# A hybrid decoder layer on one core: gate projections as fp32 products inside the attention loop, through DRAM, with three score banks

## The chip, the core and the metric

The kernel runs on one core of a Trainium2 chip. TensorE (PE) multiplies, VectorE (DVE), ScalarE (ACT) and GpSimd (POOL) do the rest, SyncE (SP) issues most of the DMA transfers. The engines run their own instruction queues in order and wait for each other on semaphores. The metric is the device time of one execution in microseconds; lower is better.

## The reference

One layer, 1024 tokens of width 1024, fp32. Two parts, each behind a modulated RMS norm and with a residual around it:

```python
# mixer: three attentions on h, merged by gates of every channel
q_a, kv_a, gate_a, qkv_b, q_c, kv_c, merge = split_cols(h @ w_in, IN_WIDTHS)
o_a = nsa_attention(...)      # 8 heads: compressed + selected + 512-token window
o_b = stick_breaking(...)     # 4 heads, all earlier keys
o_c = swa_with_sinks(...)     # 4 heads, 128-token window
g = jax.nn.sigmoid(merge).reshape(B, S, N_BRANCH, D)
y = g[:, :, 0] * (o_a @ w_branch_a) + g[:, :, 1] * (o_b @ w_branch_b) + g[:, :, 2] * (o_c @ w_branch_c)
return y @ w_out
# then: top-2 of 16 experts per token (router, gather, silu(x @ w_gate) * (x @ w_up) @ w_down, weighted sum)
```

`merge` is the product of h (1024 x 1024) with 3072 columns of w_in: the gate projection, of which this change speaks.

## The kernel before

The kernel is one program with an order written out by hand for each engine. Its stages follow each other on TensorE:

- **Projections** (0 to 337 us): norms, modulation, q, k and v of all heads. The normed tokens stay in SBUF as `hT`.
- **The attention loop** (337 to 1031 us). Queries are worked in 8 tiles of 128 tokens (n = 0 to 7). A tile has 20 units: 8 window heads (`win`, at most 5 key blocks of 128), 8 selected heads (`slc`, n+1 blocks) and 4 sliding-window heads (`swa`, at most 2 blocks). Each unit has a *slot*; 6 slots drain the loop, so there are 166. Four `sb` heads per tile (n+1 blocks) *ride* in slots 6, 9, 12 and 15, and a `cmp` unit (compressed keys) opens the tile. In slot q TensorE makes the scores of its unit and of its ride (L1631, masks L1633), then the transposes (L1660) of the unit of slot q-1 and of the ride of slot q-4, and value products (L1692) one unit behind these. VectorE takes the row maximum (L1224), ScalarE the exponential (L871), both copy the transposed probabilities out of PSUM (L387, L389). VectorE gathers a tile's output in slots 5, 10 and, for the tile before, 2 (L1196 to L1208). Scores use two PSUM buffers of two banks (512 columns each) in turn (`score_buf`, L348): a unit's scores wait until those of two units earlier have been read.
- **The mix** (1031 to 1416 us), 48 groups r = 6m + 2b + half: for 128 output channels m, branch b and half of the tokens, the gate projection and the branch product. fp32 tokens and weights of the gate are split into a high and a low fp32r part by ScalarE and VectorE (`tokens_hi`, L435; `weights_hi`, L447; L440 and L452), and TensorE makes lo*hi + hi*lo + hi*hi: 24 products a group (L1728). The branch product is plain fp32, 4 or 2 products (L1733). ScalarE's sigmoid (L908), VectorE's product and sum (L1293 to L1299) follow. The weights come in 8 loads, one per m (`loads`, from `L_MIX` on).
- **Output projection** (to 1557 us): x and the first expert weights are loaded by SP behind the mix (L565, L576), products L1758, then x1 and the second norm (L1312 on).
- **Routing** (to 1627 us): the plan of blocks, the table `slot_tok` by 16 scattering DMAs (L744) of GpSimd. SP fills the unused rows of `y_dram` with copies of x in a loop over `n_spare` (L594; 8 of them here, for 24 blocks).
- **Experts** (1627 to 2108 us), a loop over 16 experts and inside it over their blocks of 128 tokens. All products are split in three as above (L1791 to L1793 gate and up, L1831 to L1836 down). ScalarE makes the high parts of the next expert's weights (L934, six halves), VectorE the low parts (L1407, six halves); TensorE's first gate product of an expert waits for both low halves of the gate weights (L1811). After its splits VectorE copies the last block's result (L1420), then ScalarE does silu (L964) and VectorE the product with up (L1438), which is transposed (L1819).
- **Tail**: rows gathered from `y_dram`, weighted, added to x1, stored.

## Time and profile before

| | us |
|---|---|
| median of 3 runs (2157.27 to 2161.97) | 2158.88 |
| the profiled execution | 2160.99 |
| its span, first to last instruction | 2159.4 |
| attention loop, 337 to 1026: TensorE busy | 606.29 of 689 |
| mix, 1040 to 1417: TensorE busy | 375.38 of 377 |
| experts, 1627 to 2108: TensorE busy | 446.67 of 481 |

Times in rows are microseconds from the start of the span, or durations in microseconds. PE is TensorE's matmul, PEld its weight load. L is a line of the kernel. A row of a timeline names start, length, engine, line, operation, output<-input and count; behind it in brackets the idle time of that engine before it and what ended it. PEclk is the clock that was granted to TensorE as a share of 2.4 GHz; it knows that level and half of it. An fp32 product is two matmul instructions, an fp32r product one.

### The profile page before, as it was taken

To read this page: it belongs to the slowest core of one execution; us is meant where nothing else is said; L and a number is where in the kernel's file an instruction comes from. 1 tells how busy PE (TensorE), PEld (TensorE's weight loads), DVE (VectorE), ACT (ScalarE), POOL (GpSimd) and SP (SyncE) were. 2 spreads that over 40 slices of the span, in tenths; PEclk is the share of its full clock that TensorE was granted. 3 is DMA by queue.
4 is the path that set the end of the run, shared out by engine and by line. 5 is a ranking of instruction groups with operands and counts; after the bars stand their busy time and mean duration, and the time that the engine had idled before them with its cause. 6 is when DMAs were issued, how large, how long until landed. Compare 5 with 4: busy or idle time off the path is not lost.

```text
span 2159.4 us, 22519 instructions
## 1 busy us (share of the span) xinstructions
PE 1864.6 (86%) x8189; PEld 1337.2 (62%) x8189; DVE 968.5 (45%) x1519; ACT 667.7 (31%) x1168; POOL 239.3 (11%) x277
## 2 busy tenths in 40 slices
PE   2999998788989898989799999989808999999990
PEld 2554646666667676767577777745506777777770
DVE  5554314545445364645422222123353566466575
ACT  1311103333424252525311111100124445354551
POOL 3211310000101010202000000000040000000002
PEclk9999996666777696969899999999958999999995
DMA  9244310000000000000112211163344667586758
GB/s 342 101 156 137 76 43 1 1 1 1 1 1 1 1 1 1 1 1 1 39 39 65 53 40 39 40 235 114 105 131 175 226 232 280 187 308 246 267 191 321
DMA packets 119362, 226.64 MB, mean 105 GB/s; under 512 B 6888, under 2 KB 45888, under 8 KB 119136
## 3 DMA queue, kind: packets, MB, share of 16 engines
q1 hardware_dynamic: 107744, 189.50, 26.0%
q0 software_dynamic: 7920, 22.72, 3.0%
q10 hardware_dynamic: 3600, 13.11, 1.5%
q8 instruction: 61, 1.00, 0.2%
q14 instruction: 37, 0.30, 0.0%
HBM read 199.60 MB, written 29.91 MB: 106 GB/s over the span
## 4 chain that ended last, share of the span: by engine, by line
PE 73%; DVE 14%; ACT 4%; issue 4%; DMA 3%; POOL 1%; SPq 1%; ACTq 0%; DVEq 0%; POOLq 0%
PE psum L1728 12%; PE psum L1631 9%; PE psum L1532 8%; PE psum L1692 7%; PE psum L1733 5%; PE psum L1791 4%; PE psum L1793 4%; PE psum L1792 4%; PE psum L1660 4%; PE psum L1758 4%; DVE arena_r L1407 3%; PE psum L1552 3%; ACT heads_r L934 1%; DVE negm L1224 1%; POOL slot_tok L744 1%
## 5 line engine op out<-in xcount | busy, mean ns | idle before, releaser
L1692 PE MATMUL psum<-kv,arena 128*128 128x64 f32 x1464 | 229.9, 309 | 59.9 <-DVE arena L1208 36.1
L1692 PEld LDWEIGHTS psum<-kv,arena 128*128 128x128 f32 x1464 | 223.0, 231 | 67.7 <-issue 38.1
L1728 PE MATMUL psum<-arena_r,kv_r 128*128 128x512 f32 x768 | 238.3, 391 | 0.0
L1631 PE MATMUL psum<-kv,heads 112*128 112x512 f32 (+7 forms) x384 | 194.4, 620 | 9.9 <-DVE arena L1232 9.1
L1532 PE MATMUL psum<-arena 128*128 128x512 f32 (+2 forms) x512 | 187.7, 520 | 0.0
L1224 DVE TENSOR_REDUCE negm<-psum 128x1 f32<-128x640 f32 (+7 forms) x128 | 90.5, 707 | 213.0 <-PE psum L1633 212.6
L1791 PE MATMUL psum<-arena_r,kv_r 128*128 128x512 f32 x384 | 154.9, 403 | 33.9 <-DVE arena_r L1407 31.7
L1728 PE MATMUL psum<-arena_r 128*128 128x512 f32 x384 | 169.9, 442 | 9.5 <-DVE arena_r L452 9.5
L871 ACT ACTIVATE arena<-psum,negm 128x640 f32<-128x640 f32 (+7 forms) x128 | 89.7, 701 | 281.6 <-DVE negm L1224 279.9
L1660 PE MATMUL psum<-ident,arena 128*128 128x128 f32 x828 | 158.7, 321 | 15.5 <-ACT arena L387 8.9
L1728 PEld LDWEIGHTS psum<-arena_r,kv_r 128*128 128x128 f32 x768 | 145.0, 189 | 41.0 <-issue 11.2
L1793 PE MATMUL psum<-heads_r,kv_r 128*128 128x512 f32 x384 | 153.4, 399 | 0.0
L1792 PE MATMUL psum<-heads_r,kv_r 128*128 128x512 f32 x384 | 153.1, 399 | 0.0
L1407 DVE TENSOR_TENSOR arena_r<-arena,heads_r 128x2048 fp32r<-128x2048 f32 x64 | 142.4, 2287 | 15.2 <-ACT heads_r L934 15.1
L722 POOL TENSOR_SCALAR arena<-arena 128x128 f32<-128x128 f32 (+7 forms) x32 | 76.4, 2389 | 602.1 <-ACT arena L894 602.1
L1532 PEld LDWEIGHTS psum<-arena 128*128 128x128 f32 x512 | 95.5, 191 | 75.9 <-issue 73.0
L1660 PEld LDWEIGHTS psum<-ident,arena 128*128 128x128 f32 x828 | 112.9, 172 | 47.7 <-issue 20.9
L908 ACT ACTIVATE kv<-psum 128x512 f32<-128x512 f32 x48 | 28.7, 597 | 323.1 <-PE psum L1728 323.1
L934 ACT ACTIVATE heads_r<-arena 128x2048 fp32r<-128x2048 f32 x64 | 117.2, 1913 | 2.5 <-DMA arena<-in_w_exp_up_dram 1.6
L1733 PE MATMUL psum<-heads,arena 128*128 128x512 f32 x256 | 117.6, 591 | 0.0
L1758 PE MATMUL psum<-arena,bc 128*128 128x512 f32 x256 | 112.5, 599 | 2.7 <-issue 2.7
L1631 PEld LDWEIGHTS psum<-kv,heads 112*128 112x128 f32 (+1 forms) x384 | 80.7, 251 | 47.8 <-issue 35.8
(347 smaller groups left out, 2696.1 us busy)
## 6 DMA issues: line engine op xcount, KB each, us to landing
arena<-in_w_exp_gate_dram SPq DMA_DIRECT2D x16, 2048.0 KB, 9.4
arena<-in_w_exp_up_dram SPq DMA_DIRECT2D x16, 2048.0 KB, 11.9
arena<-in_w_exp_down_dram SPq DMA_DIRECT2D x16, 2048.0 KB, 10.1
arena<-in_w_ada_dram SPq DMA_DIRECT2D x7, 2048.0 KB, 15.4
y_dram<-bc ACTq DMA_DIRECT2D x25, 512.0 KB, 2.7
arena<-in_w_in_dram SPq DMA_DIRECT2D x24, 512.0 KB, 5.3
bc<-in_w_ada_dram SPq DMA_DIRECT2D x4, 2048.0 KB, 8.1
arena<-in_w_in_dram SPq DMA_DIRECT2D x3, 2048.0 KB, 11.7
```

Source lines behind the costliest of these rows:

```text
L934: act.activation(ew_hi[i][:, cs], w_raw(e, i)[:, cs], ACT.Copy).then_inc(w_hi_ok, 1)
L1407: dve.tensor_tensor(ew_lo(e, i)[:, cs], w_raw(e, i)[:, cs], ew_hi[i][:, cs].bitcast(F32), ALU.subtract).then_inc(w_lo_ok, 1)
L1532: mm = pe.matmul(psum[:, 4 + s % 3, 0:w], hT[:, k, n * P:(n + 1) * P], slot(slot_of(L_TOK + ch))[:, k, 0:w], start=(k == 0), stop=(k == NK ...
L1631: mm = pe.matmul(b[:, c0:c1], lhs, keys[:, k0 + c0:k0 + c1], start=True, stop=not masks)
L1660: ins = pe.transpose(bank[:, c * P:(c + 1) * P], src[:, t * P:(t + 1) * P], ident[:, :])
L1692: mm = pe.matmul(psum[:, bank, c * HD:(c + 1) * HD], pt[:, j * P:(j + 1) * P], v, start=(j == 0), stop=(j == u["nb"] - 1))
L1728: mm = pe.matmul(psum[:, 2 * (r % 4), :], w, h, start=(k == 0 and i == 0), stop=(k == NK - 1 and i == 2))
L1733: mm = pe.matmul(psum[:, 2 * (r % 4) + 1, :], mix_branch(s)[:, k, :], oT[:, hf * 4:(hf + 1) * 4, k, :], start=(k == k0), stop=(k == k1 - 1))
L1758: mm = pe.matmul(psum[:, 2 * (n % 2) + h, :], yT[:, k, n * P:(n + 1) * P], slot(slot_of(L_OUT + h))[:, k, :], start=(k == 0), stop=(k == N ...
L1791: pe.matmul(out, lhs_hi[:, k, :], rhs_lo(k), start=(k == 0), stop=False)
L1792: pe.matmul(out, lhs_lo[:, k, :], rhs_hi(k), start=False, stop=False)
L1793: mm = pe.matmul(out, lhs_hi[:, k, :], rhs_hi(k), start=False, stop=(k == n - 1))
```

## The change

1. **Gate projections in the loop.** The 48 gate groups are made as plain fp32 products, 8 per group, no split. `gate_steps(q)` spreads them: from slot 2 on, three slots make one group with 3, 3 and 2 products, at the end of TensorE's slot; the last group ends in slot 145. They use PSUM bank 3; ScalarE copies it to `z_stage` at the end of its slot, SP stores it to `z_dram`. Weights (512 KB per pair of groups) are loaded by SP in three buffers.
2. **Three score banks.** Bank 3 being taken, scores have banks 0 to 2. Units of up to 4 blocks take the bank used longest ago, `cmp` bank 2, larger ones banks 0 and 1 together; each waits for the last users of its banks. The ride's scores move behind the transposes and values of their slot.
3. **The mix** has branch products alone; their weights and the first half of w_out are loaded during the loop. z comes back from DRAM six groups at a time (1.5 MB) into two buffers, ScalarE makes the sigmoid of all six at once. The second half of w_out is loaded behind the loop.
4. **Expert passes** (`project_tokens`): for gate and up first all products with high weights, waiting for high halves, then those with low weights, waiting for low halves; down waits for low halves one by one.
5. **Spare rows.** All 33 blocks of `y_dram` are filled by SP during the loop; ScalarE waits for that before its first store.
6. Some semaphores go; `res_in` is shared by two loads.

```diff
+                big = u["kind"] != "cmp" and u["n"] + 1 - u["lo"] > 4
+                rest = [2] if u["kind"] == "cmp" else [min((0, 1, 2), key=lambda b: bank_user[b])]
+                u["banks"] = [0, 1] if big else rest
+                u["after"] = sorted({bank_user[b] for b in u["banks"]} - {-1})
+                for b in u["banks"]:
+                    bank_user[b] = n_s
...
         def score_buf(u):
-            return psum[:, 2 * (u["s"] % 2):2 * (u["s"] % 2) + 2, :].rearrange("p a b -> p (a b)")
+            return psum[:, u["banks"][0]:u["banks"][-1] + 1, :].rearrange("p a b -> p (a b)")
...
+        N_GATE, FILL0 = 3 * 2 * NK, 2
+        GATE_BANK = psum[:, 3, :]
+        gate_w = [part_of(0, i * NK * P, (i + 1) * NK * P).rearrange("p (k n) -> p k n", k=NK) for i in range(3)]
+        z_stage = [part_of(0, 3 * NK * P + i * BANK, 3 * NK * P + (i + 1) * BANK) for i in range(2)]
+        gate_in, branch_in = [sem(f"gate_in{i}") for i in range(3)], [sem(f"branch_in{i}") for i in range(2)]
+        g_full, z_ok = sem("g_full"), sem("z_ok")
+        z_out, z_in = [sem("z_out0"), sem("z_out1")], [sem("z_in0"), sem("z_in1")]
+
+        def gate_steps(q):
+
+            g, c = divmod(q - FILL0, 3)
+            return (g, ((0, 1, 2), (3, 4, 5), (6, 7))[c]) if 0 <= g < N_GATE else (g, ())
+
+        def branch_w(m):
+            a = m % 4 * NK * P
+            return part_of(4 + m // 4, a, a + NK * P).rearrange("p (k n) -> p k n", k=NK)
+
+        def z_group(m):
+            return part_of(2 + m % 2, 0, 6 * BANK)
...
+        z_dram = nc.dram_tensor("z_dram", [NK, P, 6 * BANK], F32, kind="Internal").ap()
...
-            load(L_MIX)
+
+            def load_gate(t):
+                m, b = divmod(t, 3)
+                sp.dma_start(gate_w[t % 3], win[:, :, C_MERGE + b * D + m * P:C_MERGE + b * D + (m + 1) * P]
+                             ).then_inc(gate_in[t % 3], 16)
+
+            sp.wait_ge(hid_full, 1)
+            for t in range(3):
+                load_gate(t)
             sp.dma_start(wr[:, :, :], w_router.rearrange("(k p) e -> p k e", p=P)).then_inc(wr_in, 16)
             sp.dma_start(rbias[:, :], router_bias.partition_broadcast(P)).then_inc(wr_in, 16)
 
+            for g in range(N_GATE):
+                sp.wait_ge(z_ok, g + 1)
+                sp.dma_start(z_dram[g // 6, :, g % 6 * BANK:(g % 6 + 1) * BANK], z_stage[g % 2]).then_inc(z_out[g % 2], 16)
+                if g % 2 and g // 2 + 3 < N_GATE // 2:
+                    load_gate(g // 2 + 3)
+                if g <= N_BLK:
+                    sp.dma_start(y_dram[g * P:(g + 1) * P, :], x2d[0:P, :]).then_inc(spare_out, 16)
+            for m in range(NK):
+                for w, k0, k1 in ((w_branch_a, 0, 4), (w_branch_b, 4, 6), (w_branch_c, 6, 8)):
+                    sp.dma_start(branch_w(m)[:, k0:k1, :], w.rearrange("l (k p) n -> p (l k) n", p=P)[:, :, m * P:(m + 1) * P]
+                                 ).then_inc(branch_in[m // 4], 16)
+            for i in range(2):
+                sp.wait_ge(z_out[i], 8 * N_GATE)
+            load(L_OUT)
+
+            def load_z(m):
+                sp.dma_start(z_group(m), z_dram[m]).then_inc(z_in[m % 2], 16)
+
             sp.wait_ge(t_full, n_g)
-            for i in range(L_MIX + 1, len(loads)):
-                load(i)
+            sp.wait_ge(pv_done, n_v)
+            load_z(0)
+            load_z(1)
+            load(L_OUT + 1)
+            for m in range(2, NK):
+                sp.wait_ge(mix_done, 6 * (m - 1))
+                load_z(m)
 
             def load_expert(e, i):
                 w = (wge, wue, wde)[i]
                 sp.dma_start(as_k(w_raw(e, i), i), w[e]).then_inc(expert_w[3 * (e % 2) + i], 16)
 
-            wait_used(sp, L_OUT - 1)
...
-            n_spare = sp.value_load(plan_i[0:1, 2 * NE + 1:2 * NE + 2], min_val=1, max_val=N_BLK - NE)
-            with sp.Fori(0, n_spare) as j:
-                sp.dma_start(y_dram[bass.ds(N_BLK * P - j * P, P), :], x2d[0:P, :]).then_inc(spare_out, 16)
...
+                sp.dma_start(res[n], x1_dram[n * P:(n + 1) * P, :]).then_inc(res_in[n // 2], 16)
...
-            tokens_hi(act, 0)
-            weights_hi(act, 0)
-            tokens_hi(act, 1)
-            weights_hi(act, 1)
-            for r in range(3 * 2 * NK):
-                if r % 2 == 0:
-                    weights_hi(act, r // 2 + 2)
-                act.wait_ge(mix_full, 2 * r + 1)
-                if r >= 2:
-                    act.wait_ge(mix_done, r - 1)
-                act.activation(sig[r % 2], psum[:, 2 * (r % 4), :], ACT.Sigmoid).then_inc(sig_ok, 1)
+                g, ks = gate_steps(q)
+                if NK - 1 in ks:
+                    act.wait_ge(g_full, g + 1)
+                    if g >= 2:
+                        act.wait_ge(z_out[g % 2], 16 * (g // 2))
+                    act.activation(z_stage[g % 2], GATE_BANK, ACT.Copy).then_inc(z_ok, 1)
+
+            for m in range(NK):
+                act.wait_ge(z_in[m % 2], 16 * (m // 2 + 1))
+                act.activation(z_group(m), z_group(m), ACT.Sigmoid).then_inc(sig_ok, 1)
...
+            act.wait_ge(spare_out, 16 * (N_BLK + 1))
...
+                sig = z_group(m)[:, r % 6 * BANK:(r % 6 + 1) * BANK]
+                dve.wait_ge(mix_full, r + 1)
+                dve.wait_ge(sig_ok, m + 1)
...
-                if u["s"] >= 2:
-                    wait_scores_read(pe, u["s"] - 2)
+                for i in u["after"]:
+                    wait_scores_read(pe, i)
...
+            def gate_matmuls(q):
+
+                g, ks = gate_steps(q)
+                t, hf = divmod(g, 2)
+                for k in ks:
+                    if k == 0:
+                        if hf == 0:
+                            pe.wait_ge(gate_in[t % 3], 16 * (t // 3 + 1))
+                        if g:
+                            pe.wait_ge(z_ok, g)
+                    mm = pe.matmul(GATE_BANK, gate_w[t % 3][:, k, :], hT[:, k, hf * BANK:(hf + 1) * BANK],
+                                   start=(k == 0), stop=(k == NK - 1))
+                    if k == NK - 1:
+                        mm.then_inc(g_full, 1)
+
             waiting = None
-            for s in slots:
+            for q, s in enumerate(slots):
                 for u in s["S"]:
-                    scores(u)
+                    if u is not s["ride"]:
+                        scores(u)
                 for u in s["T"]:
                     if waiting and "v" not in u:
                         values(waiting)
@@ -1705,32 +1707,25 @@
                     if waiting:
                         values(waiting)
                     waiting = u if "v" in u else None
+                if s["ride"]:
+                    scores(s["ride"])
+                gate_matmuls(q)
...
+            pe.wait_ge(z_ok, N_GATE)
             for r in range(3 * 2 * NK):
                 m, b, hf = r // 6, r // 2 % 3, r % 2
-                s = slot_of(L_MIX + m)
-                if r % 6 == 0:
-                    wait_load(pe, L_MIX + m)
+                if r % 24 == 0:
+                    pe.wait_ge(branch_in[m // 4], 16 * 12)
                 if r >= 4:
                     pe.wait_ge(mix_done, r - 3)
-                pe.wait_ge(w_rest, r // 2 + 1)
-                if r < 2:
-                    pe.wait_ge(h_rest, r + 1)
-                for k in range(NK):
-                    w_hi, w_lo = gate_hi(r // 2)[:, k, :], gate_lo(r // 2)[:, k, :]
-                    t_hi, t_lo = (h[:, k, hf * BANK:(hf + 1) * BANK] for h in (h_hi, h_lo))
-                    for i, (w, h) in enumerate(((w_lo, t_hi), (w_hi, t_lo), (w_hi, t_hi))):
-                        mm = pe.matmul(psum[:, 2 * (r % 4), :], w, h, start=(k == 0 and i == 0),
-                                       stop=(k == NK - 1 and i == 2))
-                mm.then_inc(mix_full, 1)
                 k0, k1 = ((0, 4), (4, 6), (6, 8))[b]
                 for k in range(k0, k1):
-                    mm = pe.matmul(psum[:, 2 * (r % 4) + 1, :], mix_branch(s)[:, k, :],
+                    mm = pe.matmul(psum[:, 2 * (r % 4) + 1, :], branch_w(m)[:, k, :],
...
-            def split_matmuls(out, lhs_hi, lhs_lo, rhs_hi, rhs_lo, n):
-
-                for k in range(n):
-                    pe.matmul(out, lhs_hi[:, k, :], rhs_lo(k), start=(k == 0), stop=False)
-                    pe.matmul(out, lhs_lo[:, k, :], rhs_hi(k), start=False, stop=False)
-                    mm = pe.matmul(out, lhs_hi[:, k, :], rhs_hi(k), start=False, stop=(k == n - 1))
-                return mm
+            def project_tokens(i, e, w_hi, w_lo, full):
+
+                out, c0 = psum[:, i, :], 6 * e + 2 * i
+                for k in range(NK):
+                    if k % 4 == 0:
+                        pe.wait_ge(w_hi_ok, c0 + k // 4 + 1)
+                    pe.matmul(out, xs_hi[:, k, :], w_hi[:, k, :], start=(k == 0), stop=False)
+                    pe.matmul(out, xs_lo[:, k, :], w_hi[:, k, :], start=False, stop=False)
+                for k in range(NK):
+                    if k % 4 == 0:
+                        pe.wait_ge(w_lo_ok, c0 + k // 4 + 1)
+                    mm = pe.matmul(out, xs_hi[:, k, :], w_lo[:, k, :], start=False, stop=(k == NK - 1))
+                mm.then_inc(full, 1)
...
-                    for i, full in enumerate((gate_full, up_full)):
-                        pe.wait_ge(w_lo_ok, 6 * e + 2 * i + 2)
-                        split_matmuls(psum[:, i, :], xs_hi, xs_lo, lambda k: hi[i][:, k, :], lambda k: lo[i][:, k, :],
-                                      NK).then_inc(full, 1)
+                    project_tokens(0, e, hi[0], lo[0], gate_full)
+                    project_tokens(1, e, hi[1], lo[1], up_full)
...
-                    pe.wait_ge(w_lo_ok, 6 * e + 6)
                     for k in range(4):
                         if k % 2 == 0:
+                            pe.wait_ge(w_lo_ok, 6 * e + 5 + k // 2)
```

## Rows read from the trace of the kernel before

**Rows 1.** The page: busy time, share and instructions of each engine.

```profile
PE 1864.6 (86%) x8189; PEld 1337.2 (62%) x8189; DVE 968.5 (45%) x1519; ACT 667.7 (31%) x1168; POOL 239.3 (11%) x277
```

**Rows 2.** Table of stretches: length, busy us (count) by engine, PEclk, DMA, GB/s.

```profile
337.00:1026.00 689.00, 606.29 (x3228) 465.97 (x3228) 340.72 (x703) 274.24 (x640) 78.24 (x40) 0.77 0.00 1
1040.00:1417.00 377.00, 375.38 (x1415) 266.57 (x1416) 85.47 (x104) 50.40 (x71) 0.00 (x0) 1.00 0.16 40
1627.00:2108.00 481.00, 446.67 (x2016) 360.11 (x2016) 282.41 (x259) 237.73 (x239) 36.67 (x48) 0.98 0.65 236
```

**Rows 3.** Waits in the loop: us in total, times, longest.

```profile
PE psum L1692 <- DVE arena L1208: 36.1, 7, 5.3
PE psum L1692 <- DVE arena L389: 23.8, 19, 2.8
```

**Rows 4.** Tile 6: a timeline row, then a stretch as in rows 2.

```profile
819.31 2.37 PE L1692 MATMUL psum<-kv,arena 128*128 128x64 f32 x10 [5.27 <-DVE arena L1208]
832.00:836.00 4.00, 4.00 (x26) 3.94 (x25) 1.52 (x2) 1.05 (x3) 0.00 (x0) 0.62 0.02 6
```

**Rows 5.** Chain that ended last, in the mix: start, us, what.

```profile
1047.32 3.43 PE psum L1733 x8
1050.75 5.45 PE psum L1728 x24
```

**Rows 6.** Timeline near the loop's end, tile 7.

```profile
1014.29 1.22 DVE L1274 TENSOR_TENSOR arena<-arena 128x1024 f32<-128x1024 f32 x1
1018.06 1.23 DVE L1224 TENSOR_REDUCE negm<-psum 128x1 f32<-128x1024 f32 x1 [1.36 <-PE psum L1633]
1018.09 1.90 PE L1692 MATMUL psum<-kv,arena 128*128 128x64 f32 x16
1019.32 1.11 ACT L871 ACTIVATE arena<-psum,negm 128x1024 f32<-128x1024 f32 x1 [0.97 <-DVE negm L1224]
```

**Rows 7.** Timeline from the loop into the mix, and behind the mix.

```profile
1030.65 3.62 ACT L435 ACTIVATE arena_r<-arena 128x4096 fp32r<-128x4096 f32 x1 [0.26 <-PE psum L1660]
1040.11 0.76 PE L1728 MATMUL psum<-arena_r 128*128 128x512 f32 x1 [9.50 <-DVE arena_r L452]
1043.72 0.40 PE L1728 MATMUL psum<-arena_r 128*128 128x512 f32 x1
1422.64 29.16 PE L1758 MATMUL psum<-arena,bc 128*128 128x512 f32 x64 [2.67 <-issue]
1446.43 1.23 DVE L1312 TENSOR_TENSOR heads<-psum,ga_bc 128x1024 f32<-128x1024 f32 x1 [25.13 <-DMA kv<-in_x_dram]
```

**Rows 8.** The page's DMA issues: KB each, us to landing.

```profile
bc<-in_w_ada_dram SPq DMA_DIRECT2D x4, 2048.0 KB, 8.1
```

**Rows 9.** Timeline of the routing: scatters and splits.

```profile
1584.45 8.90 DVE L1407 TENSOR_TENSOR arena_r<-arena,heads_r 128x2048 fp32r<-128x2048 f32 x4
...
1587.92 1.86 POOL L744 DMA_INDIRECT slot_tok<-tok_id,dest  x1 [0.30 <-issue]
...
1600.16 0.96 POOL L744 DMA_INDIRECT slot_tok<-tok_id,dest  x1 [0.30 <-issue]
```

**Rows 10.** Experts: chain that ended last, then timeline.

```profile
1701.00 1.93 ACT heads_r L934
1723.13 1.93 ACT heads_r L934
1921.69 1.93 ACT heads_r L934
1942.13 1.93 ACT heads_r L934
...
1729.72 0.47 PE L1791 MATMUL psum<-arena_r,kv_r 128*128 128x512 f32 x1 [2.11 <-DVE arena_r L1407]
1739.68 0.60 ACT L964 ACTIVATE bc<-psum 128x512 f32<-128x512 f32 x1 [5.14 <-DVE bc L1420]
1740.90 0.75 DVE L1438 TENSOR_TENSOR bc<-bc,psum 128x256 f32<-128x256 f32 x2 [1.91 <-PE psum L1793]
```

85 lines of the change are left out of this document (15 added, 70 removed).

## Prediction

> **What bounds the kernel now.** I read the page first: TensorE is busy 86% of the span [rows 1]. A busy share says little about an engine whose clock changes, so the second view is the table of stretches [rows 2]. Three stretches hold 1547 of the 2159.4 us. The reader should see the pair of figures in each: in the mix (1040 to 1417) TensorE is busy 375.4 of 377 us at a granted clock of 1.00, so it is bound by the number of its products alone. In the attention loop (337 to 1026) it is busy 606.3 of 689 us, but at a mean of 0.77: it sits idle 82.7 us, and for a large part of the rest runs at the lower of its two levels. The experts (1627 to 2108) are busy 446.7 of 481 us at 0.98. So work taken out of the mix comes off the end in full, and work put into the loop can hide in two places, idle time and the slow clock.
>
> **The attention loop, as it stands.** The granted clock has two levels, 2.4 and 1.2 GHz, so busy time times mean clock is about the work at full clock: 606.3 x 0.77 = 467 us. If all the idle time fell at the lower level, the busy part would have a clock of 0.81 and the work would be 489 us; I take 467. The loss to the clock is then 606 - 467 = 139 us. The third view, the waits, says what ends the idle time: 36.1 us in 7 waits of the value products for VectorE's gather (L1208), 23.8 us for its copies out of PSUM [rows 3]; the rest is spread thin. The gather's wait is one of some 5.3 us at the start of each of tiles 1 to 7, and after it TensorE keeps the lower level for long: the 4 us from 832 on have a mean of 0.62, so it came back at about 835 [rows 4].
>
> **What the change adds to the loop.** 48 gate groups of 8 fp32 products of 512 columns are 384 products. The mix's branch products are of the same shape and type: four products of branch A are 8 instructions, so two each, and the 8 go by in 3.43 us [rows 5]. 768 instructions x 3.43/8 = 329 us at full clock. (The products they replace are 1152 single-pass ones, 24 in 5.45 us, 262 us [rows 5]: on TensorE the new form is 67 us dearer.) Loop work becomes 467 + 329 = 796 us.
> *Idle time.* The gather's waits stay (36 us): the values that wait stand in slot 2 behind that slot's scores, and the gate products are queued behind the values, in an engine that keeps its order. Of the other 47 us I let half stay: a gate step stands between the transposes of one slot and the values of the next and so covers copies, and the compressed scores have a bank of their own; waits inside a slot are not covered. The new waits: from tile 4 on a unit of more than 4 blocks takes banks 0 and 1 together, so its scores wait until the exponential of the large unit before has read them. In tile 7 the maximum starts at 1018.06 and the exponential ends at 1020.43, 2.4 us [rows 6]. The slot's values alone take 1.9 us there (its transposes come on top), and the gate step adds 8/3 x 0.86 = 2.3 us, so the chain is covered. The gate steps end with slot 145 of 166; in the last 14 loaded slots only the four ride units, whose reader comes right behind them, are bare: 4 x 1.3 = 5 us. Sum 36 + 24 + 5 = 65 us.
> *Clock.* Each slot gets 2.3 us of dense products. In the mix, after 9.5 us of idleness, dense products had the upper level back by 1043.7, in 3.6 us or less [rows 7]; in the loop it took some 15 us after 819.3 [rows 4]. I price 8 tiles at 4 us lost each, 32, and 3 for the first tile: 35 us. Bounds: 0, and 139 x 796/467 = 238 us, if the shares stay as they are. I take the low side, since a slot would be dense for a third to three quarters of its time.
> ScalarE gets 48 copies of 0.6 us and VectorE nothing; both are at half load (340.7 and 274.2 of 689 us). SyncE's queue, idle in the loop, gets stores, weight loads and 33 spare copies, about 42 MB in 800 us, behind no one's deadline: a weight buffer is read again six groups later. Loop: 796 + 65 + 35 = 896 us for 689, **+207**.
>
> **What it takes from the mix.** Before: from 1026 to 1416.1 are 390 us: the last gather and transposes until 1031, splits of tokens and weights until 1040.1 [rows 7], then the products. After: 5 us until 1031, then 256 branch instructions x 0.429 = 110 us [rows 5], 2 us for a slow start, 1.5 us for VectorE behind the last: 118.5. The read-back has to keep this up. Two z groups of 1.5 MB and a half of w_out are issued as the loop ends; 2 MB take 8.1 us to land [rows 8], and a sigmoid of 3072 columns is 3/4 of the 3.62 us of a 4096-column copy [rows 7], plus 1.3 us for its table. So VectorE starts 10 to 12 us after the loop, and TensorE has four groups (10 us) to do ahead of it. Later each buffer has 13.7 us for 8 + 2.7 us. Covered, with little to spare; if not, each group costs up to 3 us, 20 in all. Mix: **-271** (-250 if bare).
>
> **Behind the mix.** The second half of w_out was issued when the mix was through and held the first output product until 1422.6, 2.7 us after TensorE was free; x, queued behind it and four expert loads, came at 1446.4 [rows 7]. With w_out already there, both come sooner: **-6** (0 to -8).
>
> **Spare rows early.** They leave the path between routing and the experts. The scatters of slot_tok are issued there, 1.9 us each until 1598, then 0.96 [rows 9]. Two things end at about 1598: the spare copies and VectorE's six splits, which began at 1584.5 and take 13.4 us at 8.9 for four. If the copies are the cause, 7 us go; if the splits are, none: **-2** (0 to -7). [...]
>
> **Experts.** TensorE waits 2.1 us for the low halves (L1407) at each of 15 changes of expert, as at 1729.7 [rows 10], and some changes are followed by a dip of the clock: one-block experts take 22.1 us with it (1701.00 to 1723.13) and 20.4 without (1921.69 to 1942.13) [rows 10]. The new order needs only the high halves at first, so the 2.1 us go. But what is late next is VectorE: its six splits are followed by its copy of the last result, then ScalarE's silu (1739.68 to 1740.28), then the product L1438. At 1740.90 that product waited for TensorE, but silu was only some 0.6 us ahead [rows 10]. ScalarE and VectorE alone need 17.3 us from L934 (1723.13) to a ready silu (1740.3), plus 2.8 to the next L934: some 20 us for 20.4. So 0.4 us x 15 = 6, and half of the dips, of which 5 of the 14 intervals seem to hold one, at 1.7 us, 4: **-10** (-3 to -30; the full 2.1 us and all dips would be 40, but the chain excludes it). The tail is unchanged (0; +1 for the paired waits on res).
>
> **Sum.** 207 - 271 - 6 - 2 - 10 = -82. The profiled execution took 2160.99 us (span 2159.4), 2.1 above the median of the runs, so 2079 for it and **2077 us** as a median.
>
> **Rivals.**
> *A, better filled loop.* The gate steps also take most of the slow clock (10 instead of 35) and half of the remaining waits (15 less): 2077 - 40 = 2037. For it: dense work at 1.00 in the mix. Against: the gather's waits, longer than a step.
> *B, single-buffered scores, slower.* Tiles 4 to 7 have 64 + 16 large units. If VectorE is still in a scan when scores end (scan and subtraction before 1015.4 take some 3.5 us, of which the subtraction alone is 1.2 [rows 6]), the chain is not 2.4 but up to 5.9 us. It cancels the 82 us from 1.03 us a unit on; at 1.8 us it gives 2077 + 144 = 2221. Against: 5 us of TensorE work per slot between two scores in all but the last 14.
> *C, the clock does not rise.* Loss 238 instead of 35: 2280; it cancels the gain from 117 us on. Partly so (80): 2122.
> *D, the experts gain nothing or the read-back is bare*: up to +30, 2107.
> A change that does not do what it says would be an expert stage at 481 us with its waits only renamed; that is D.
>
> **How the numbers follow.** Forecast (with D) 0.67, A 0.2, C in part 0.06, C in full 0.02, B 0.05. The range reaches to A's time and to C in part with D's smaller half: 2030 to 2130; it leaves out some 0.15. A measurement of this kernel can tell about 0.2%, 4 us. Faster 0.92 (forecast, A, C in part, less 0.01), same 0.01, slower 0.07 (B and C in full).
>
> **What would show it.** Right: the loop some 207 us longer with a clock of 0.93 to 0.97 in it; gate instructions at 0.43 us; mix stretch of some 115 us with TensorE busy throughout; seven waits for L1208 still of 5 us; in the experts L1407 gone from TensorE's waits and L1438 (or its product's transposes) in its place. Wrong: waits of score products for ScalarE's L871 in tiles 4 to 7 of over 1 us (B), a clock under 0.87 in the loop (C), gaps of TensorE in the mix every 13.7 us (read-back).

## The result and the profile after

| | before | after |
|---|---|---|
| median, us | 2159.24 (2157.27 to 2161.97, 4 runs) | 2127.02 (2117.63 to 2131.74, 4 runs) |
| profiled execution, us | 2160.99 | 2127.09 |
| its span, us | 2159.4 | 2125.4 |
| attention loop | 694.2 (337.1 to 1031.3) | 946.5 (335.2 to 1281.7) |
| mix, from the loop's end | 384.8 (to 1416.1) | 113.6 (to 1395.3) |

The ratio is 0.984 (95% interval 0.9823 to 0.9856): 32 us faster where 82 were forecast. The time lies in the range given; the gain is 50 us smaller than forecast.

The page's first group of the kernel after:

```profile
PE 1852.2 (87%) x7805; PEld 1195.6 (56%) x7805; DVE 933.9 (44%) x1493; ACT 659.6 (31%) x1150; POOL 239.5 (11%) x277
```

The table of stretches of [rows 2] in the kernel after (length, busy us and count of PE, PEld, DVE, ACT, POOL, then PEclk, DMA share, GB/s):

```profile
335.00:1276.00 941.00, 859.69 (x3996) 537.34 (x3996) 342.41 (x705) 302.36 (x688) 78.62 (x40) 0.94 0.17 51
1281.00:1395.00 114.00, 111.83 (x256) 49.20 (x256) 55.41 (x81) 22.90 (x9) 0.00 (x0) 0.98 0.35 129
1601.00:2075.00 474.00, 444.77 (x2016) 363.47 (x2016) 282.83 (x259) 238.06 (x239) 36.58 (x48) 0.97 0.66 240
```

TensorE's total busy time hardly moved from [rows 1], 1864.6 to 1852.2 us, with 384 fewer instructions. The loop's row is the one to read. It is 941 us where the forecast had 896, and it still has 81 us without a product, as before (82.7, [rows 2]).

The waits of TensorE in that loop (us in total, times, longest), to be read against [rows 3]:

```profile
PE psum L1678 <- DVE arena L1199: 36.7, 7, 5.3
PE psum L1678 <- DVE arena L394: 20.0, 15, 2.1
PE psum L1646 <- ACT arena L392: 6.9, 12, 0.9
PE psum L1617 <- ACT arena L888: 5.2, 4, 1.6
PE psum L1617 <- ACT arena L865: 5.1, 4, 1.3
PE psum L1678 <- ACT arena L392: 5.1, 10, 0.7
```

L1678 are the value products (L1692 before), L1199 the gather (L1208), L394 and L392 the copies of probabilities out of PSUM by VectorE (L389) and ScalarE, L1617 the scores, L865 ScalarE's exponential and L888 its copy of a ride's scores. Both rows of before are there again almost unchanged: 36.1 became 36.7, 23.8 became 20.0. Behind them are the two new rows of L1617, 10 us in 8 waits of scores for the reader of their bank, 1.3 us each in the mean: the four of L888 are all in tile 7, those of L865 come once in each of tiles 4 to 7. Two rows of the kernel before belong beside them:

```profile
PE psum L1631 <- DVE arena L1232: 9.1, 8, 2.0
PE psum L1660 <- ACT arena L387: 8.9, 7, 1.4
```

The first is a wait of scores for VectorE's reading of the compressed scores; it is all but gone (0.6 us). The second is the wait of transposes for ScalarE's copies, 6.9 us after, with 5.1 us of value products waiting for the same copies behind it. All waits for copies together were 33.5 us and are 32.0. The last tile, where steps stand only in the first 6 of 20 slots, has the longest idle time and the lowest clock:

```profile
1137.37:1281.68 144.31, 123.84 (x663) 86.37 (x661) 62.56 (x103) 51.67 (x91) 18.31 (x12) 0.87 0.17 50
```

The stretches add up in the two profiled executions: start of the loop -2, loop +252, mix -271, output stage -3, routing -2, experts -8, tail 0, together -34 us.

### The profile page after: what moved, and what is told of

Same layout as the page of the kernel before. It is cut to its first block, busy times and chain, and to the rows that moved or that the text cites. A ratio compares the mean times of both kernels' runs of the same rounds, so it can differ in the third digit from the quotient of the medians.

```text
span 2125.4 us, 21714 instructions
## 1 busy us (share of the span) xinstructions
PE 1852.2 (87%) x7805; PEld 1195.6 (56%) x7805; DVE 933.9 (44%) x1493; ACT 659.6 (31%) x1150; POOL 239.5 (11%) x277
## 4 chain that ended last, share of the span: by engine, by line
PE 70%; DVE 16%; issue 4%; ACT 3%; DMA 3%; POOL 1%; ACTq 1%; SPq 1%; DVEq 0%; POOLq 0%
PE psum L1692 17%; PE psum L1518 9%; PE psum L1617 8%; DVE arena_r L1393 8%; PE psum L1678 7%; PE psum L1728 5%; PE psum L1753 4%; PE psum L1646 4%; PE psum L1538 3%; PE psum L1789 2%; PE psum L1790 2%; PE psum L1794 2%; ACT heads_r L924 1%; POOL slot_tok L740 1%; DVE negm L1215 1%
## 5 line engine op out<-in xcount | busy, mean ns | idle before, releaser
L1692 PE MATMUL psum<-arena 128*128 128x512 f32 x768 | 387.2, 640 | 0.5 <-ACT arena L894 0.4
L1678 PE MATMUL psum<-kv,arena 128*128 128x64 f32 x1464 | 198.1, 280 | 61.9 <-DVE arena L1199 36.7
L1678 PEld LDWEIGHTS psum<-kv,arena 128*128 128x128 f32 x1464 | 188.4, 201 | 69.5 <-issue 38.2
L1692 PEld LDWEIGHTS psum<-arena 128*128 128x128 f32 x768 | 144.7, 204 | 128.3 <-issue 128.0
L865 ACT ACTIVATE arena<-psum,negm 128x640 f32<-128x640 f32 (+7 forms) x128 | 89.6, 700 | 404.5 <-DVE negm L1215 404.5
L1617 PE MATMUL psum<-kv,heads 112*128 112x512 f32 (+7 forms) x384 | 147.9, 490 | 5.8 <-ACT arena L888 5.2
L1646 PE MATMUL psum<-ident,arena 128*128 128x128 f32 x828 | 131.3, 280 | 10.6 <-ACT arena L392 6.9
L1518 PEld LDWEIGHTS psum<-arena 128*128 128x128 f32 x512 | 95.5, 191 | 75.8 <-issue 73.0
L1617 PEld LDWEIGHTS psum<-kv,heads 112*128 112x128 f32 (+1 forms) x384 | 73.2, 202 | 90.7 <-issue 84.0
L1646 PEld LDWEIGHTS psum<-ident,arena 128*128 128x128 f32 x828 | 92.5, 146 | 41.5 <-issue 27.2
L1794 PE MATMUL psum<-arena_r,kv_r 128*128 128x512 f32 x384 | 95.0, 389 | 0.0
L1728 PEld LDWEIGHTS psum<-heads,arena 128*128 128x128 f32 x256 | 49.2, 193 | 63.2 <-issue 63.2
L1789 PEld LDWEIGHTS psum<-heads_r,kv_r 128*128 128x128 f32 x384 | 72.9, 190 | 17.8 <-DVEq L1411 2.6
## 6 DMA issues: line engine op xcount, KB each, us to landing
arena<-in_w_exp_up_dram SPq DMA_DIRECT2D x16, 2048.0 KB, 12.3
```

What stands on the lines that cost most here:

```text
L1518: mm = pe.matmul(psum[:, 4 + s % 3, 0:w], hT[:, k, n * P:(n + 1) * P], slot(slot_of(L_TOK + ch))[:, k, 0:w], start=(k == 0), stop=(k == NK ...
L1617: mm = pe.matmul(b[:, c0:c1], lhs, keys[:, k0 + c0:k0 + c1], start=True, stop=not masks)
L1646: ins = pe.transpose(bank[:, c * P:(c + 1) * P], src[:, t * P:(t + 1) * P], ident[:, :])
L1678: mm = pe.matmul(psum[:, bank, c * HD:(c + 1) * HD], pt[:, j * P:(j + 1) * P], v, start=(j == 0), stop=(j == u["nb"] - 1))
L1692: mm = pe.matmul(GATE_BANK, gate_w[t % 3][:, k, :], hT[:, k, hf * BANK:(hf + 1) * BANK], start=(k == 0), stop=(k == NK - 1))
L1728: mm = pe.matmul(psum[:, 2 * (r % 4) + 1, :], branch_w(m)[:, k, :], oT[:, hf * 4:(hf + 1) * 4, k, :], start=(k == k0), stop=(k == k1 - 1))
```

## Experiments

All were timed beside the kernel before, whose median was there between 2160.6 and 2163.6 us. Differences from the kernel after are taken from the medians of separate runs; where one is only a few us, the traces have to bear it out.

### 1. The score banks alone

The kernel before with three banks for scores instead of four and the ride's scores behind the values, and nothing else of the change:

```
- return psum[:, 2 * (u["s"] % 2):2 * (u["s"] % 2) + 2, :]
+ return psum[:, u["banks"][0]:u["banks"][-1] + 1, :]
- if u["s"] >= 2: wait_scores_read(pe, u["s"] - 2)
+ for i in u["after"]: wait_scores_read(pe, i)
```

> One part alone, on the kernel before: three score banks (large units take banks 0 and 1 together) and the ride's scores behind transposes and values; no gate products in the loop, mix and experts as before. Theory T (the loop's idle time stayed because the waits stand inside a slot, ahead of its gate step; the banks themselves cost little): the loop of 694 us grows by 10 to 20 us, with new waits of scores for L871 and L894 copies of about 1 us each in tiles 4 to 7; 2170 to 2180 us. Rival R1 (single-buffered large scores are what ate the 45 us that the loop is longer than forecast): the loop grows by 40 us or more, 2200 us.

Measured: 2189.59 us (2187.58 to 2197.0), ratio 1.0125 (1.0094 to 1.0155): 26 us slower (32 us in the profiled loops). Its loop as one stretch:

```profile
338.34:1064.60 726.26, 632.84 (x3236) 479.88 (x3236) 344.28 (x709) 274.85 (x641) 78.62 (x40) 0.75 0.00 1
```

Its waits of scores for the ride's copy (L901) and the exponential (L878):

```profile
PE psum L1638 <- ACT arena L901: 18.3, 16, 1.6
PE psum L1638 <- ACT arena L878: 4.5, 8, 0.8
```

That lies between T's 10 to 20 us and R1's 40. R1's cause, large units waiting for the exponential, is 4.5 us here and 5.1 us in the kernel after, so it is not what ate the 45 us. The same 3236 instructions as before take 632.8 us instead of 607.8: 726.3 - 632.8 = 93 us are idle, 7 more than before (86; the new waits are 23 us, but the 9.1 us for the compressed scores and some of those for copies are gone), and the other 25 lie in the busy time, at a clock of 0.75 instead of 0.77. Busy time times clock is 475 for 468 us, within what two decimals of the clock leave open, so most of the 25 us is the clock. This execution is the slowest of the four, and how much of the 25 us is its own is not shown. Without the gate products the three banks are a loss of 26 us; in the change's own loop only 10 us of such waits are left.

### 2. The banks without the ride's move

As 1, but the ride's scores at their old place:

```
- for u in s["S"]:
-     if u is not s["ride"]: scores(u)
+ for u in s["S"]: scores(u)
...
- if s["ride"]: scores(s["ride"])
```

> The kernel before with three score banks, but with the ride's scores left at their old place, ahead of the transposes (the other kernel with three banks moved them behind the slot's values, and took 2189.6 us, 26 us over the kernel before). Theory T (the number of banks is what costs: a ride must wait until the scores of a slot or two before have been read, and its place within the slot changes little): 2184 to 2196 us, about 20 waits of TensorE for the exponentials of ScalarE with some 20 us in the loop. Rival R1 (moving the ride is the cost): 2163 to 2175 us. Rival R2 (the place behind the values is what keeps the cost low: ahead of the transposes the wait is longer by the time of transposes and values, some 3 us per ride of the longer tiles): 2210 us or more.

Measured: 2209.42 us (2201.38 to 2213.27), ratio 1.0229 (1.0212 to 1.0246), 20 us above experiment 1, above T and next to R2's 2210. The waits, and the loop as one stretch:

```profile
PE psum L1638 <- ACT arena L901: 27.0, 16, 2.3
PE psum L1638 <- ACT arena L878: 9.1, 9, 1.8
...
336.22:1066.00 729.78, 617.39 (x3233) 473.65 (x3234) 344.37 (x709) 273.69 (x640) 78.21 (x40) 0.76 0.00 1
```

36 us in 25 waits instead of 23 us in 24: the place of the ride matters in R2's direction, but by 0.5 us a wait where R2 had some 3. The idle time is 112 us, 26 more than before, and the busy time 10 us more: here idle time brought less slow clock with it than in experiment 1. The profiled executions of the two are only 4 us apart (2199.7 and 2195.4 us), so of the 20 us between the medians I call only the direction and the waits shown.

### 3. A step inside the slot where the gather is awaited

The kernel after with a whole group of eight gate products in slot 2 of tiles 1 to 7, between the transposes and the values that wait for the gather; the other steps stay at the end of their slots and start again in slot 3 of each tile:

```
+ steps[t0 + 2] = (gq, tuple(range(8)))
...
+ early = last_values >= 0 and (s["i"] == 2)
+ for i, (f, u) in enumerate(calls):
+     if early and i == last_values: gate_matmuls(q)
+     f(u)
```

> The changed kernel with the gate steps redistributed: in slot 2 of tiles 1 to 7 a whole group of 8 products stands between the transposes and the values that wait for VectorE's gather; the other groups in three slots each as before; the last group is in slot 2 of tile 7. Same products, same order otherwise. Theory T: 6.9 us of products cover the wait of 5.3 us, so the seven waits for the gather (36.7 us) go, and the dips of the clock behind them too (some 3 to 4 us each): loop 50 to 60 us shorter, 2127 becomes 2070 to 2080. Rival R2 (VectorE's and ScalarE's chain behind the gather sets the tile's start, so the wait comes back one slot later): at most 10 us shorter, 2117 or more.

Measured: 2067.21 us (2063.37 to 2073.63), ratio 0.9556 (0.9527 to 0.9585): 60 us less than the kernel after, for the same instructions in another order; this is T. The seven waits of 5.3 us are gone from its list; of the gather only the wait at the loop's end is left:

```profile
PE psum L1662 <- DVE arena L1215: 3.3, 1, 3.3
...
PE psum L1694 <- DVE arena L394: 20.6, 16, 2.1
```

### 4. All steps inside their slots

As 3, and the ordinary steps too stand ahead of the slot's last values, in every slot without a ride:

```
- early = last_values >= 0 and (s["i"] == 2)
+ early = last_values >= 0 and (s["i"] == 2 or not s["ride"])
```

> This kernel is the one whose group of eight gate products stands in slot 2 of each tile ahead of the last values (it took 2067.2 us, its loop 891.7 us with 49.6 us idle on TensorE). Here the ordinary gate steps too stand ahead of the slot's last values, in every slot without a ride, where before they stood at the slot's end. Theory T (the idle time that the change left in the loop lies inside the slots, ahead of where its steps stand, so the place of a step decides and not the amount of work): of the waits for evacuated probability groups in that loop (20.6 us in 16 by VectorE, 6.9 and 5.4 us by ScalarE) about half goes, 15 to 20 us; idle in the loop 30 to 37 us, time 2045 to 2055 us. Rival R: a step ahead of the values delays the values and with them the next slot's evacuation and exponentials, so that waits come back elsewhere: idle 45 us or more, time 2064 us or more.

Measured: 2026.98 us (2025.4 to 2028.47), ratio 0.9379 (0.9363 to 0.9394): another 40 us, twice what T gave it. The wait for VectorE's copies:

```profile
PE psum L1694 <- DVE arena L394: 2.7, 3, 1.7
```

Tile 5 as a stretch, in the kernel after:

```profile
857.09:993.11 136.02, 125.55 (x617) 81.10 (x616) 51.12 (x93) 45.34 (x92) 12.56 (x4) 0.96 0.10 30
```

In experiment 3:

```profile
843.59:972.52 128.93, 123.51 (x623) 79.66 (x621) 51.14 (x93) 45.37 (x92) 12.57 (x4) 1.00 0.11 31
```

And in experiment 4:

```profile
804.25:930.30 126.05, 122.96 (x623) 80.16 (x623) 51.14 (x93) 45.03 (x92) 12.56 (x4) 1.00 0.11 32
```

The work (busy times clock) is 121, 124 and 123 us; the first has a third of a gate group less in it, 2.3 us. What goes is idle time, 10.5, 5.4 and 3.1 us. The slow clock goes with the gather's wait: the clock is 1.00 already in experiment 3, with 5.4 us of short gaps still there. Over the whole loop, each term summed tile by tile from such rows (the loss is busy time less work):

| us | loop | idle | lost to the clock | work |
|---|---|---|---|---|
| before | 694.2 | 86 | 140 | 467 |
| after | 946.5 | 85 | 52 | 810 |
| 3 | 891.7 | 50 | 31 | 811 |
| 4 | 853.3 | 26 | 25 | 803 |

Of the 93 us between the kernel after and experiment 4, 59 are idle time, 27 are clock and 7 are in the work column, which the clock's two decimals leave uncertain by about as much. In tiles 0 to 6 idle time falls from 64 to 12 us and the loss to the clock from 35 to 5. Tile 7 keeps 13 us idle and 20 us of loss; it takes 133.7 us in this execution, 127.5 in that of experiment 3 and 125.2 in that of experiment 10, which has the same loop as this one.

### 5. ScalarE's store behind the SiLU

The kernel after, with the wait for VectorE's copy of the block's result, and the store, moved behind `silu` (the order that results):

```
  act.activation(y_sb[:, BANK:D], psum[:, 6, :], ACT.Copy).then_inc(y_act, 1)
+ act.wait_ge(gate_full, j + 2)
+ act.activation(silu_g, psum[:, 0, :], ACT.Silu).then_inc(silu_ok, 1)
  act.wait_ge(y_act, j + 1)
  act.wait_ge(y_dve, j + 1)
  act.dma_start(y_dram[bass.ds(j * P, P), :], y_sb).then_inc(y_out, 16)
```

> The changed kernel, with ScalarE's store of a block's result (and its wait for VectorE's copy) moved behind silu in the experts. Theory T (ScalarE's and VectorE's chain from the high halves through six splits, VectorE's copy, silu and the product with up sets a one-block expert's 20.0 us): silu no longer follows VectorE's copy, the chain is 1.1 us shorter, one-block experts take 18.9 to 19.2 us, and with the stall of TensorE under 1 us its clock dips less: stage of 473 us becomes 450 to 458, 2127 becomes 2105 to 2112. Rival (TensorE's own work or the weights' arrival sets the period): 20.0 us stay, 2127.

Measured: 2098.73 us (2096.42 to 2102.77), ratio 0.9713 (0.9682 to 0.9745): 28 us less: T's mechanism, and more than T's 2105 to 2112 gave it. A change of expert in the kernel after, timelines of ScalarE and VectorE:

```profile
1685.87 0.59 ACT L934 ACTIVATE bc<-psum 128x512 f32<-128x512 f32 x1
1691.13 0.34 ACTq L937 DMA_DIRECT2D y_dram<-bc  x1
1691.59 0.60 ACT L955 ACTIVATE bc<-psum 128x512 f32<-128x512 f32 x1 [5.13 <-DVE bc L1406]
...
1690.21 0.69 DVE L1406 COPY bc<-psum 128x512 f32<-128x512 f32 x1
1692.30 0.75 DVE L1424 TENSOR_TENSOR bc<-bc,psum 128x256 f32<-128x256 f32 x2 [1.41 <-ACT bc L955]
```

TensorE's wait behind it, of the transposes of the product:

```profile
PE psum L1818 <- DVE bc L1424: 26.8, 15, 2.2
```

The same place in the kernel of this experiment:

```profile
1681.70 0.58 ACT L934 ACTIVATE bc<-psum 128x512 f32<-128x512 f32 x1
1682.17 0.60 ACT L957 ACTIVATE bc<-psum 128x512 f32<-128x512 f32 x1
...
1686.05 0.68 DVE L1410 COPY bc<-psum 128x512 f32<-128x512 f32 x1
1686.65 0.74 DVE L1428 TENSOR_TENSOR bc<-bc,psum 128x256 f32<-128x256 f32 x2
```

And the wait:

```profile
PE psum L1822 <- DVE bc L1428: 6.6, 15, 0.8
```

ScalarE sat idle for 5.13 us with the gate product ready, because the store ahead of `silu` in its queue waited for VectorE, which was at its six splits. With `silu` first, VectorE goes from its copy straight to the product. From the first split of one expert to that of the next it now takes 18.45 us instead of 20.0 with one block, and 36.6 instead of 38.05 with two; four intervals of two blocks were 39.5 to 40.0 us in the kernel after, none is here. That is some 1.5 us at each of 15 changes and some 1.6 more at four of them, 29 us for the 28 measured.

### 6. The old order of the expert passes

The kernel after with each product waiting for both low halves and going low, mixed, high; the down product too waits for both its low halves again:

```
+ pe.wait_ge(w_lo_ok, c0 + 2)
  for k in range(NK):
+     pe.matmul(out, xs_hi[:, k, :], w_lo[:, k, :], start=(k == 0), stop=False)
...
```

> The changed kernel with the expert passes in their old order: each product of a token block waits for both halves of the weights' remainders, and goes low, mixed, high per contraction step. In the changed kernel the expert stage is some 8 us shorter than before. Theory T (the order of the passes gave those 8 us, by moving TensorE from the wait for VectorE's split of the weights, 31.7 us in 15, to a wait for VectorE's product of the activations, 26.8 us in 15): 2132 to 2138 us, with the 15 waits for the split back. Rival R (it is within the spread of the runs, and the stage is set by VectorE and ScalarE around the token block): 2124 to 2130 us.

Measured: 2136.2 us (2131.11 to 2140.17), ratio 0.988 (0.9843 to 0.9917): 9 us more, T's time. By the medians alone the 9 us are hardly clear of the two intervals, but the traces agree: from the second expert's first split of weights to the last expert's it takes 421.5 us, as in the kernel before (421.7), and 413.6 in the kernel after. The wait of [rows 10] is back:

```profile
PE psum L1788 <- DVE arena_r L1393: 31.5, 15, 2.1
```

### 7. The store's place in the kernel before

The edit of 5 in the kernel before:

```
+ act.activation(silu_g, psum[:, 0, :], ACT.Silu).then_inc(silu_ok, 1)
  act.wait_ge(y_act, j + 1)
  act.wait_ge(y_dve, j + 1)
  act.dma_start(y_dram[bass.ds(j * P, P), :], y_sb).then_inc(y_out, 16)
- act.wait_ge(gate_full, j + 2)
- act.activation(silu_g, psum[:, 0, :], ACT.Silu).then_inc(silu_ok, 1)
```

> The kernel before with one edit, ScalarE's store of a token block's output moved behind the SiLU (in the changed kernel the same edit was worth 28 us). Theory T (the passes' order and the store's place hide one another: with the old order the expert's first block waits for VectorE's split of the weights, so the store's place is worth less): 5 to 15 us less than the kernel before, 2145 to 2155 us. Rival R1 (the two are independent): 2131 to 2136 us. Rival R2 (worth nothing with the old order): 2158 to 2163 us.

Measured: 2160.77 us (2156.04 to 2165.86, 10 runs), ratio 1.0003 (0.9986 to 1.002): nothing, R2. The timelines at a change of expert:

```profile
1733.69 0.60 ACT L966 ACTIVATE bc<-psum 128x512 f32<-128x512 f32 x1 [0.92 <-PE psum L1797]
...
1739.13 0.75 DVE L1442 TENSOR_TENSOR bc<-bc,psum 128x256 f32<-128x256 f32 x2 [1.93 <-PE psum L1797]
```

`silu` now starts 12.3 us after the first high copy (1721.35) instead of 16.6 (1723.13 to 1739.68, [rows 10]). But the product L1442 starts 15.8 us after the first split (1723.31), as it did before (1725.08 to 1740.90): it waits for TensorE's up product (L1797), which the wait for the low halves holds up. So T's 5 to 15 us are not there. The order of the passes is worth some 9 us with the store at its old place; the store's move is worth nothing with the old order and 28 us with the new one, because it hid behind the wait for the low halves.

### 8. The scatters without VectorE beside them

The kernel after with VectorE's splits of the first expert held until all scatters have landed:

```
+ dve.wait_ge(table_ok, 16 * 2 * NT)
  expert_weights_lo(0)
```

> The changed kernel, with VectorE's six splits of expert 0 held back until the 16 scatters of slot_tok have landed. Theory P (VectorE's two-input splits slow GpSimd's scatters; the spare copies, gone from there, did not): all scatters at a pitch of 1.26 us instead of 2.2 us for the first six, table ready 5 to 6 us earlier, 2127 becomes 2121 to 2123. Rival (the first scatters are slow by themselves): pitch unchanged, and the splits, now later, cost 0 to 5 us, 2127 to 2132.

Measured: 2116.3 us (2111.72 to 2122.36), ratio 0.9782 (0.975 to 0.9813): P's mechanism, 5 us below its range. GpSimd's scatters in the kernel after:

```profile
1564.20 1.86 POOL L740 DMA_INDIRECT slot_tok<-tok_id,dest  x1 [0.31 <-issue]
1566.37 1.90 POOL L740 DMA_INDIRECT slot_tok<-tok_id,dest  x1 [0.30 <-issue]
```

And in this one, with the load of the first block's indices and its gather:

```profile
1561.22 0.96 POOL L740 DMA_INDIRECT slot_tok<-tok_id,dest  x1 [0.30 <-issue]
1562.48 0.96 POOL L740 DMA_INDIRECT slot_tok<-tok_id,dest  x1 [0.30 <-issue]
...
1582.71 0.61 POOL L746 DMA_DIRECT2D idx<-slot_tok  x1 [4.08 <-issue]
1585.94 3.03 POOL L753 DMA_INDIRECT kv<-xn_dram,idx  x1 [2.62 <-DMA idx<-slot_tok]
```

In the kernel after the scatters beside the splits keep the pitch of 2.2 us of [rows 9], although the spare copies are no longer beside them. It is the pitch of the splits (8.90 us for four): one scatter a split. Without the splits all sixteen take 0.96 to 1.12 us, and the last begins 6.5 us earlier from the first. The splits now run from 1581.41 to 1594.7: the gather among them takes 3.03 us instead of 0.99, but the load of its indices, also among them, 0.61 us as without them. This settles what the prediction left open: the splits were the cause, the copies were not. The Trainium skill, page "SBUF — State Buffer", section "SBUF: two separate sides", says that VectorE operations with two SBUF inputs lock the port pair they share with GpSimd only against GpSimd operations that read SBUF. The trace agrees: scatters and gathers take their indices from SBUF (`dest`, `idx`) and are slowed, the load, which reads DRAM alone, is not. By the traces the hold is worth 4.7 us (the spans), by the medians 10.7, whose intervals do not exclude the smaller figure.

### 9. x ahead of the expert weights

The kernel after with the first two loads of x ahead of four expert loads in SyncE's queue:

```
+ load_x(0)
+ load_x(1)
  for i in range(3): load_expert(1, i)
  load_expert(0, 2)
```

> The changed kernel with one edit: the first two tiles of x are loaded ahead of the four expert loads that stand before them in SyncE's queue. In the changed kernel the first of them landed 18.8 us after its issue at 1402.1 us, and VectorE waited 20.8 us for it after the mix. Theory T (the load waits behind 8 MB of expert weights): it lands in 3 to 6 us, the stage from the end of the mix to the last router product shrinks by 12 to 16 us, time 2110 to 2116 us. Rival R (what follows the first tile, the router's chain of 16.3 us per pair, or the expert weights that now come later, sets the end): 2122 to 2130 us.

Measured: 2123.59 us (2122.37 to 2125.76), ratio 0.9824 (0.9808 to 0.9841): 3.4 us less, R. That alone would not be clear of the spread, but in the traces the stage from the mix's last result to the last router product takes 141.2 us instead of 145.0. In the kernel after, VectorE's first use of x, and TensorE behind it:

```profile
1421.02 1.23 DVE L1298 TENSOR_TENSOR heads<-psum,ga_bc 128x1024 f32<-128x1024 f32 x1 [20.84 <-DMA kv<-in_x_dram]
1428.27 1.78 PE L1763 MATMUL psum<-ident,kv 128*128 128x128 f32 x8 [1.95 <-DVE kv L1311]
1429.84 14.94 PE L1753 MATMUL psum<-arena,bc 128*128 128x512 f32 x32
```

In this one:

```profile
1414.95 1.22 DVE L1304 TENSOR_TENSOR heads<-psum,ga_bc 128x1024 f32<-128x1024 f32 x1 [12.50 <-PE psum L1759]
1428.43 1.04 PE L1769 MATMUL psum<-ident,kv 128*128 128x128 f32 x8
```

x comes in time, and VectorE waits for TensorE instead, which makes output products for two tiles (27.6 us) before anyone needs the result. A wait of 20.8 us on an engine off the path was worth 3.8 us, what TensorE itself had lost by it: 1.95 us of idleness, 0.7 us in the slower transposes behind (1.78 for 1.04) and 1.0 in the next 32 products (14.94 for the 13.90 of the later tiles).

### 10. The edits together

Experiment 4 with 5, 8 and 9, all on the kernel after:

```
+ early = last_values >= 0 and (s["i"] == 2 or not s["ride"])
+ expert_store(j)                            # behind silu
+ dve.wait_ge(table_ok, 16 * 2 * NT)
+ load_x(0); load_x(1)
```

> The changed kernel with four edits together: gate steps inside the slots (the whole group in slot 2, the others ahead of the last values), ScalarE's expert store moved behind the SiLU (alone 28 us less), VectorE's first splits held until the scatters are done (alone 11 us less), and the first two tiles of x loaded ahead of the expert weights. The parts lie in four stages that follow one another. Theory T (the gains add): 2067 - 28 - 11 - 12, less 15 if the steps inside the slots help: 2000 to 2020 us. Rival R (the expert stage gives a part back, because the weights, now loaded later and wanted sooner, come last): 2030 us or more, with waits for expert loads in the expert stage that the changed kernel doesn't have.

Measured: 1996.66 us (1992.11 to 2000.7), ratio 0.9242 (0.9222 to 0.9262), 130 us below the kernel after and 165 below the one before; T, a little below its range, and TensorE waits for no load of weights in the experts, as R would have it. Its loop:

```profile
335.01:1186.00 850.99, 823.45 (x4004) 525.82 (x4005) 344.86 (x710) 302.83 (x690) 78.61 (x40) 0.97 0.19 56
```

The parts would add up to 2027 - 28 - 11 - 3 = 1985; 12 us are missing. Some 7 of them are the hold, counted at 11 and worth 4 by the traces, as the next experiment shows.

### 11. Without the hold

Experiment 10 less the edit of 8:

```
- dve.wait_ge(table_ok, 16 * 2 * NT)
```

> The kernel with all four edits (1996.7 us) less one: VectorE's first splits of the expert weights are not held until the scatters are done. The same hold alone took 10.7 us off the changed kernel's time by the rounds, but 4.7 us by the profiled executions, in which the first gather begins 6.9 us earlier and the second 4.6 us. Theory T (the hold is worth what the traces show, because the splits it delays come next and the second gather only moves by 4.6 us): 2000 to 2003 us, the scatters' pitch back at 2.2 us for the first six. Rival R (it is worth the 11 us of the rounds): 2006 us or more. Rival R2 (nothing, the held splits cost what the scatters gain): 1994 to 1998 us.

Measured: 2006.0 us (1996.68 to 2007.35), ratio 0.9275 (0.9237 to 0.9313): R's time, with single runs from T's side to R's. From the first scatter to the first gather it takes 33.1 us instead of 26.7, but from there to the end 503.2 instead of 505.5: by the traces the hold is worth 6.4 - 2.3 = 4 us. The rest lies in the loop, where tile 7 of this execution is 133.7 us long, and 125.2 in experiment 10, with the same instructions. So T's size is right for the mechanism, and two executions of the same loop differ by 7 us; a difference of that size in the loop is not a result by itself.

### 12. Gate steps for the last tile

Experiment 10 with every sixth step left out in tiles 1 to 4, and three groups more in tile 7:

```
+ n_g3 = (6, 5, 5, 5, 5, 6, 6, 3)[n_]
+ if n_ == NT - 1: free = free[::2]
+ elif n_g3 == 5: free = [q_ for i_, q_ in enumerate(free) if i_ % 6 != 5]
```

> The kernel with all four edits (1996.7 us; loop 851.0 us, of which 27.6 us idle and 19.2 us lost to the clock, 15.2 and 8.8 us of these in tile 7, which has gate steps only in its slot 2), with one more: tiles 1 to 4 leave every sixth gate step out, and tile 7 gets three groups of gate products in every second slot from its third. Theory T (a slot without a gate step is where idle time and the slower clock live, and tiles 1 to 4 have steps to spare): tile 7 gets 8 to 10 us of its 24 us back, tiles 1 to 4 give 2 to 4 us; time 1988 to 1993 us. Rival R (the spared slots show their own waits again, some 1.3 us each in 12 slots and a slower clock after them): 1997 us or more.

Measured: 1998.63 us (1995.96 to 2003.68), ratio 0.9252 (0.9219 to 0.9286): no gain, R's time. Yet up to the mix's first product its loop is 844.6 us, 6.4 shorter, about as T says. But the mix behind it:

```profile
1182.78 13.49 PE L1764 MATMUL psum<-heads,arena 128*128 128x512 f32 x24 [1.44 <-DMA arena<-in_w_branch_c_dram]
1202.54 101.44 PE L1764 MATMUL psum<-heads,arena 128*128 128x512 f32 x232 [6.26 <-DVE bc L1306]
```

SyncE's queue in front of it:

```profile
1136.97 35.32 SPq L557 DMA_DIRECT2D z_dram<-arena  x2
1172.33 0.44 SPq L564 DMA_DIRECT2D arena<-in_w_branch_a_dram  x1
```

The last gate groups now end late, their stores hold SyncE's queue until 1172.3, and the 24 weight loads, half of w_out and the read-back of z queue up behind them: 7.7 us of idle time at the start of the mix, which is 9.4 us longer from its first product on (122.7 for 113.3), so that loop and mix together are 3 us longer. Neither theory had this; the loop's gain was handed back by a queue.

## Why the prediction was right and wrong

**The loop (+207, measured +252).** This is the step that failed: 45 of the 48 us by which the stretches fall short of the forecast are in it. The prediction had a gate step "between the transposes of one slot and the values of the next" cover the waits for copies, and priced the slow clock that remains at 4 us a tile. The steps covered next to none of the copies, and the clock cost more, above all in the tile that has few steps. The three terms, over the stretch of 941 us:

- *Work, 796 forecast, 808 measured* (859.7 x 0.94). Six gate instructions follow each other in 2.58 us in experiment 4, 0.43 each, as forecast. The clock's two decimals allow 4 us. Part of the rest may be in the 467 us of the kernel before: in experiment 4 tiles 1 to 6 run at 1.00, so their busy time is their work, and without the gate products it is 359 us where the rows of the kernel before give 356. The rest stays open.
- *Idle time, 65 forecast, 81 measured.* The gather's 36 us stayed, as forecast. "Of the other 47 us I let half stay" was wrong: besides the gather's 37 and the banks' 10 there are 34 left. Most of the 13 that went are the compressed scores' wait (9.1 to 0.6 us), as their own bank promised; the waits for copies only went from 33.5 to 32.0. The reason is in the code that the prediction itself describes. The steps stand at the end of a slot; the copies are awaited inside it, by transposes and values ahead of the step. Experiments 3 and 4 show it: the same products ahead of the waiting instruction take 59 us of idle time out.
- *Clock, 35 forecast, 52 measured.* The clock rose to 0.94, in the band given (0.93 to 0.97). Tiles 0 to 6 lose 35 us where 31 were priced; tile 7 loses 16 where 4 were, with steps in 6 of its slots and 20.5 us idle. In experiment 4 27 us came back with the 59 of idle time. Not every gap costs clock: its tiles 4 to 6 have 3 us idle each at 1.00.

**The banks.** I priced the new waits at 5 us, for the four bare rides of tile 7; these cost 5.2. The other 5.1 us, one wait of 1.3 us for an exponential in each of tiles 4 to 7, were not forecast. They are the sign given for rival B, but 4 times in 80 large units, so B did not come. Without gate products between the scores the three banks cost 26 us (experiment 1), and 48 with the ride at its old place (experiment 2).

**Rival A** (idle time and clock filled by the steps, 2037) is not what the change does, but what its products can do when they stand elsewhere: experiment 4 has 2027. I had kept the gather out of its reach "longer than a step"; a whole group, 16 instructions of 0.43 us, is 6.9 us and covers all 5.3.

**The mix (-271, measured -271).** Right, with its mechanism: 111.83 of 114 us are busy. ScalarE's wait there:

```profile
ACT arena L898 <- DMA arena<-z_dram: 72.0, 8, 11.5
```

It is the read-back seen from ScalarE: it waits in all 8 groups, 72 us in all, and TensorE never for it. The margin is thin, as said: experiment 12 used it up.

**Output stage (-6, measured -3).** x was still late (20.8 us of waiting on VectorE). Experiment 9 shows that making it early would have given no more than 3.4.

**Spare rows (-2, measured -2).** The range of 0 to -7 hung on which of two things slowed the scatters. It was the splits (experiment 8), so moving the copies took nothing off the scatters themselves; the load of the indices behind the last one starts 3.3 us after it instead of 5.4.

**Experts (-10, measured -8).** L1407 went from TensorE's waits (31.7 us) and the product of the activations came in its place (26.8 us), as the last section of the prediction asked; experiment 6 gives 9 us by the medians and 8 by the traces. What the prediction's chain did not see is that its own lower bound, "some 20 us for 20.4", held a SiLU standing behind a store that waits for VectorE. It said which instruction is late next, but not what that one stands behind; experiment 5 took 28 us there.
